# Before the expert rounds, GpSimd takes the last 512 of 2048 columns of the low-part subtraction that VectorE did alone

## What is computed

```python
def swiglu(h, w_gate, w_up, w_down):
    return (jax.nn.silu(h @ w_gate) * (h @ w_up)) @ w_down
```

## Time and profile before

| | |
|---|---|
| median of 3 runs | 2388.21 us (2387.69 to 2388.84) |
| span of the profiled execution | 2388.6 us |
| PE, DVE, ACT, POOL busy | 86%, 70%, 51%, 3% of the span |
| TensorE clock granted, mean | 0.915 of full speed |
| expert rounds begin | at about 1340 us |

### The profile page before, as it was taken

One profiled execution on the slowest core, in us unless ns is written; L12 is line 12 of the kernel. 1 busy time (PEld: TensorE's weight loads), 2 busy tenths in 40 slices (PEclk: granted clock), 3 DMA queues, 4 the chain that ended last, 5 costly groups with the idle time before them and its releaser, 6 DMA issues.

```text
span 2388.6 us, 26417 instructions
## 1 busy us (share of the span) xinstructions
PE 2044.1 (86%) x9364; PEld 1689.2 (71%) x9364; DVE 1672.2 (70%) x2143; ACT 1229.4 (51%) x1401; POOL 75.3 (3%) x112
## 2 busy tenths in 40 slices
PE   4876964868887878999875799999999999999998
PEld 3665853656665757888674687878878787878787
DVE  4764596565855574444464688878888888878787
ACT  3442112553443343344361476767677676767675
POOL 0200000120200100000000000000000000000000
PEclk8888986869987869999897799999999999999999
DMA  5430340412341423555441498989999898989795
GB/s 205 157 124 18 124 137 19 149 53 71 124 140 35 142 71 118 182 193 192 126 141 36 165 377 294 378 303 368 330 344 372 298 376 297 373 297 377 288 374 206
DMA packets 235620, 499.97 MB, mean 209 GB/s; under 512 B 9308, under 2 KB 41182, under 8 KB 235414
## 3 DMA queue, kind: packets, MB, share of 16 engines
q1 hardware_dynamic: 235024, 497.09, 58.9%
q10 hardware_dynamic: 518, 1.87, 0.2%
HBM read 497.88 MB, written 1.05 MB: 209 GB/s over the span
## 4 chain that ended last, share of the span: by engine, by line
PE 73%; DVE 18%; ACT 4%; issue 2%; POOL 1%; DMA 1%; SPq 0%; ACTq 0%; DVEq 0%; POOLq 0%
PE psum L732 22%; PE psum L734 22%; PE psum L733 22%; DVE arena L1493 4%; DVE low L717 3%; PE psum L2265 1%; ACT high L714 1%; PE psum L2349 1%; POOL small L909 1%; PE psum L2315 1%; DVE small L1147 1%; PE psum L1408 1%; DVE hT_low L894 1%; PE psum L2240 1%; ACT h L1095 1%
## 5 line engine op out<-in xcount | busy, mean ns | idle before, releaser
L717 DVE TENSOR_TENSOR low<-raw,high 128x2048 fp32r<-128x2048 f32 (+2 forms) x461 | 1049.0, 2281 | 435.1 <-ACT high L714 433.6
L714 ACT ACTIVATE high<-raw 128x2048 fp32r<-128x2048 f32 (+2 forms) x461 | 877.9, 1910 | 571.6 <-PE psum L734 511.1
L732 PE MATMUL psum<-high,yT_high 128*128 128x512 f32 x1672 | 676.3, 405 | 103.2 <-DVE yT_low L1527 46.4
L734 PE MATMUL psum<-high,yT_low 128*128 128x512 f32 x1672 | 665.6, 398 | 0.0
L733 PE MATMUL psum<-low,yT_high 128*128 128x512 f32 x1672 | 665.4, 398 | 0.0
L732 PEld LDWEIGHTS psum<-high,yT_high 128*128 128x128 f32 x1672 | 323.9, 194 | 181.7 <-issue 50.6
L734 PEld LDWEIGHTS psum<-high,yT_low 128*128 128x128 f32 x1672 | 323.5, 193 | 69.4
L733 PEld LDWEIGHTS psum<-low,yT_high 128*128 128x128 f32 x1672 | 324.5, 194 | 63.6
L732 PE MATMUL psum<-high,hT_high 128*128 128x512 f32 (+2 forms) x560 | 223.4, 399 | 43.1 <-DVE h L1355 19.7
L733 PE MATMUL psum<-low,hT_high 128*128 128x512 f32 (+2 forms) x560 | 220.4, 393 | 0.0
L734 PE MATMUL psum<-high,hT_low 128*128 128x512 f32 (+2 forms) x560 | 220.2, 393 | 0.0
(11 more groups left out here) (273 smaller groups left out, 1740.1 us busy)
## 6 DMA issues: line engine op xcount, KB each, us to landing
raw<-in_moe_w_gate SPq DMA_DIRECT2D x112, 1024.0 KB, 5.2
raw<-in_moe_w_up SPq DMA_DIRECT2D x112, 1024.0 KB, 5.4
raw<-in_moe_w_down SPq DMA_DIRECT2D x112, 1024.0 KB, 5.0
raw<-in_a_w_in SPq DMA_DIRECT2D x32, 1024.0 KB, 5.4
raw<-in_ffn_w_gate SPq DMA_DIRECT2D x14, 1024.0 KB, 5.1
raw<-in_ffn_w_up SPq DMA_DIRECT2D x14, 1024.0 KB, 5.1
raw<-in_ffn_w_down SPq DMA_DIRECT2D x14, 1024.0 KB, 4.9
raw<-in_b_w_in SPq DMA_DIRECT2D x12, 1024.0 KB, 5.0
```

Of the source, the lines that this page charges most:

```text
L714: eng.activation(high, raw, ACT.Copy).then_inc(k.high_ready, 1)
L717: eng.tensor_tensor(low, raw, high.bitcast(F32), ALU.subtract).then_inc(k.low_ready, 1)
L732: pe.matmul(out, lhs.high, rhs.high, start=start, stop=False)
L734: return pe.matmul(out, lhs.low, rhs.high, start=False, stop=stop)
```

## The change

`POOL_COLUMNS = 512`. Ahead of the rounds DVE subtracts the columns 0 to n - 512 of a granule of n columns and signals `low_ready`; POOL subtracts the last 512 and signals the new `low_end_ready`. Both wait for ACT's `high_ready`. PE waits for both signals ahead of a granule, and SyncE for both ahead of a load into the same raw buffer. POOL's programme gets calls of `ahead` at the same steps as ACT's and DVE's, in every layer but moe. In the rounds `split` keeps `end=0`, all columns on DVE.

```diff
 def ahead(k, eng, name):
-    engine = "act" if eng is k.nc.scalar else "dve"
+    engine = "act" if eng is k.nc.scalar else "pool" if eng is k.nc.gpsimd else "dve"
...
-            split(k, eng, n % SPLIT, g % RAW, granule.shape[0] * granule.shape[1], granule.number)
+            split(k, eng, n % SPLIT, g % RAW, granule.shape[0] * granule.shape[1], granule.number, POOL_COLUMNS)

-def split(k, eng, slot, raw_slot, n, number):
+def split(k, eng, slot, raw_slot, n, number, end=0):
     high, low, raw = k.high[:, slot, 0:n], k.low[:, slot, 0:n], k.raw[:, raw_slot, 0:n]
     if eng is k.nc.scalar:
         eng.activation(high, raw, ACT.Copy).then_inc(k.high_ready, 1)
+    elif eng is k.nc.gpsimd:
+        eng.wait_ge(k.high_ready, number + 1)
+        eng.tensor_tensor(low[:, n - end:], raw[:, n - end:], high[:, n - end:].bitcast(F32), ALU.subtract).then_inc(k.low_end_ready, 1)
     else:
         eng.wait_ge(k.high_ready, number + 1)
-        eng.tensor_tensor(low, raw, high.bitcast(F32), ALU.subtract).then_inc(k.low_ready, 1)
+        eng.tensor_tensor(low[:, 0:n - end], raw[:, 0:n - end], high[:, 0:n - end].bitcast(F32), ALU.subtract).then_inc(k.low_ready, 1)

 def wait_split(k, pe, g):
     pe.wait_ge(k.low_ready, k.granules[g].number + 1)
+    pe.wait_ge(k.low_end_ready, k.granules[g].number + 1)

@@ sync_weights
                 sp.wait_ge(k.low_ready, before.number + 1)
+                sp.wait_ge(k.low_end_ready, before.number + 1)

@@ load_round
         sp.wait_ge(k.low_ready, round_number(k, i - RAW, t) + 1)
+        if i < RAW:
+            sp.wait_ge(k.low_end_ready, round_number(k, i - RAW, 0) + 1)

 def norm_pool(k, pool, n):
     pool.wait_ge(k.ms_ready, 2 * n + 2)
     inverse_root(k, pool, k.ms, k.rstd, k.rstd_ready)
+    ahead(k, pool, ("norm", n, 3))

 def a_pool(k, pool, j):
     for i in range(8):
...
+        ahead(k, pool, (layer, "product", i))
         pool.wait_ge(k.group_ms_ready, n + 1)
...
+    for i in range(8, 16):
+        ahead(k, pool, (layer, "product", i))
+    ahead(k, pool, (layer, "scores", 0))

+def out_pool(k, pool, layer):
+    for name in out_names(layer):
+        ahead(k, pool, name)
```

More of the change, by code:

```diff
@@ L71 @@
 GROUP = 4
+POOL_COLUMNS = 512
 VECTOR_ROWS = {}
@@ L445, in __init__ @@
         self.engine_steps = {}
-        self.split_so_far = {"act": 0, "dve": 0}
+        self.split_so_far = {"act": 0, "dve": 0, "pool": 0}
         def sb(name, shape, dtype=F32):
@@ L522, in __init__ @@
         self.low_ready = sem("low_ready")
+        self.low_end_ready = sem("low_end_ready")
         self.half_done = sem("half_done")
@@ L1224, in attention_pool @@
             inverse_root(k, pool, k.out_ms[:, 0:GROUP], k.out_rstd[:, 0:GROUP], k.out_rstd_ready)
+    out_pool(k, pool, layer)
 def a_buffers(k, j):
@@ L1366, in a_pool @@
 def a_pool(k, pool, j):
+    layer = f"a{j}"
     for i in range(8):
-        n = GROUP_MS[f"a{j}"] + i
+        n = GROUP_MS[layer] + i
+        ahead(k, pool, (layer, "product", i))
         pool.wait_ge(k.group_ms_ready, n + 1)
         inverse_root(k, pool, k.group_ms[:, 8 * (i % 4):8 * (i % 4 + 1)], k.group_rstd[:, 8 * (i % 4):8 * (i % 4 + 1)], k.group_rstd_ready)
-    attention_pool(k, pool, f"a{j}")
+    for i in range(8, 16):
+        ahead(k, pool, (layer, "product", i))
+    ahead(k, pool, (layer, "scores", 0))
+    attention_pool(k, pool, layer)
 def b_buffers(k):
@@ L1739, in c_pool @@
     for kind, i in c_order():
+        ahead(k, pool, ("c", kind, i))
         if kind in ("low", "q", "kv"):
@@ L1745, in c_pool @@
             n += 1
+    ahead(k, pool, ("c", "scores", 0))
+    out_pool(k, pool, "c")
 def h_buffers(k):
@@ L1889, in h_pool, with b_pool, ffn_pool, r_pool @@
 def h_pool(k, pool):
[L1890 to L1893, removed]
+    n = 0
+    for kind, i in h_order():
+        ahead(k, pool, ("h", kind, i))
+        if kind in ("q", "kv"):
+            groups = H_HEADS if n < 2 else H_KV_HEADS
+            pool.wait_ge(k.group_ms_ready, GROUP_MS["h"] + n + 1)
+            inverse_root(k, pool, k.group_ms[:, 8 * n:8 * n + groups], k.group_rstd[:, 8 * n:8 * n + groups], k.group_rstd_ready)
+            n += 1
+    ahead(k, pool, ("h", "scores", 0))
+    out_pool(k, pool, "h")
+def b_pool(k, pool):
+    for i, kind, pair in b_products():
+        ahead(k, pool, ("b", "product", i))
+    ahead(k, pool, ("b", "squares"))
+    out_pool(k, pool, "b")
+def ffn_pool(k, pool):
+    for kind, j, t in ffn_order():
+        if kind != "down":
+            ahead(k, pool, ("ffn", kind, j, t))
+    out_pool(k, pool, "ffn")
+def r_pool(k, pool):
+    for kind, i in r_order():
+        ahead(k, pool, ("r", kind, i))
+    out_pool(k, pool, "r")
 def ffn_buffers(k):
@@ L2552, in _ @@
                     a_pool(k, pool, int(layer[1]))
-                elif layer in ("c", "h"):
-                    {"c": c_pool, "h": h_pool}[layer](k, pool)
+                elif layer != "moe":
+                    {"b": b_pool, "c": c_pool, "h": h_pool, "ffn": ffn_pool, "r": r_pool}[layer](k, pool)
 def store(k, sp, layers):
```

## The result

The changed kernel took 2401.16 us (median of 4 runs, 2400.56 to 2401.64) against 2388.24 us: 1.0053 times the kernel before, with a 95% interval of 1.0038 to 1.0067. Five later runs of the same kernel gave 1.0039 times (1.0026 to 1.0053). So it is slower by 0.4 to 0.5%, about 11 us. The forecast of 2395 had the sign and missed the median by 6 us, nearly as much as the loss that it forecast; the range of 2379 to 2408 held it.

What follows compares the result with a forecast made beforehand. The prediction saw TensorE busy for 86% of the span with 73% of the last chain, and 22 affected subtractions on the chain. Its place terms summed to +7 us on the 2388.21 median: 2395 us, range 2379 to 2408.

Steps and rivals of the forecast that it cites:

- free: Rival: DVE and POOL share nothing at this width, all 22 subtractions on the chain gain 0.53 us: -11, 2377 us; chance 0.10.
- (a): Attention layers a0 and a1, single subtraction, then reduction, then root, three on the chain in each: +0.1 us each, +0.6.
- (b): Pair of subtractions in a0 and its twin in a1: POOL subtracts while DVE still rotates, +1.4 us each, +2.8.
- (c): The subtraction ahead of each attention, where what follows reads PSUM: -0.5 us each, -1.0.
- (d): The subtraction ahead of a1's rope tables, which have two inputs: -0.53 + 1.25 = +0.7 us.
- (h): Two subtractions at the end of the feed-forward layer, each shorter by 0.53 us: -1.1.
- (e): Three subtractions of the convolution layer, inside an unbroken run of two-input taps: +3.7 - 1.6 = +2.1 us.
- (f): Latent attention: two stalled roots behind POOL's own subtraction, +0.7 us each, and -0.5 for a single one: +0.9.
- (g): Hybrid layer, its three subtractions: 0, +0.7 and about +0.2 us, +0.9 in the sum.
- (i): Recurrent layer: a conversion ends within the scan and product sequence leading to the output products: +1.2 us.
- One-sided: Rival: POOL waits for DVE, never DVE for POOL: about -6, 2382 us; chance 0.19.
- slow POOL: Rival: POOL takes 2.3 us an operation, some 19 places pay 1.05 us more each: +20 more, 2415 us; chance 0.12.

Runs made afterwards that it cites:

- pool_memset: The changed kernel, but POOL sets its 512 columns to zero without reading, waits kept, those low parts left out: 2377.52 us, 0.9946 times the kernel before.
- no_a: The changed kernel with the subtractions of the attention layers a0 and a1 given back whole to DVE: 2391.78 us, 1.0002 times the kernel before.
- only_b: The kernel before, with only the three subtractions inside the convolution layer's taps divided between DVE and POOL: 2390.96 us, 1.0008 times the kernel before.
- pool_extra: The changed kernel, but DVE subtracts all 2048 columns and POOL also the last 512, into its own buffer: 2411.29 us, 1.0089 times the kernel before.
- changed_again: The changed kernel word for word, run for a second profiled execution: 2400.9 us, 1.0039 times the kernel before.
- w1024: The changed kernel with 1024 columns on POOL, or half of a narrower granule, in place of 512: 2419.18 us, 1.0122 times the kernel before.

## Why the prediction was right in sign and 6 us off

**Part 1, DVE's gain.** The size is right, 0.53 us an operation, and the free case was put at -11: pool_memset, which is that case with all waits kept, is at -12.9. But the count of 22 places came near the total by luck. In c, with one place counted (0.5 us), the layer is 4.7 us shorter in pool_memset, with TensorE granted 0.85 of full speed there against 0.81 before; b, with three places (1.6), is 1.8 longer.

**Part 2, POOL's own time.** 1.25 us taken, 1.27 to 1.30 measured where POOL is first. The upper end of 2.3 is out. The estimate of 1.1 us from the Trainium skill, "GPSIMD Engine Reference", section "Performance versus the Vector engine", is lower than these rows, and equals what POOL needs behind DVE (2.87 less 1.76).

**Part 3, both ways.** The row that spoke against (a power passed by DVE's product) was rightly overruled. POOL first stops DVE for nearly its whole length: 2.88 us for 1.76. The order was right in most places, DVE first by 0.04 us; but in four (56.89, 449.92, 606.97 and 808.06) POOL was first by 0.02 to 0.03 with both idle, which I had excluded. Each costs DVE 1.1 us there.

**(a) and (b), the step that failed.** I put "Single subtraction, then reduction, then root (three on the chain in each of the layers a0 and a1)" at +0.1 each and let POOL be first only at "the pair at 66.64 and its twin in a1". The timeline shows POOL first, inside a rotation, at 614.61 (two), 628.03, 643.07 and 657.78 in a1, and at 64.50 (two), 77.90, 93.23 and 107.95 in a0: an item of these layers has two subtractions, and the conversion of the first is long done when POOL leaves its roots. The chain of before had shown only DVE's unbroken work there, so I had counted the second of each item and not the first. Each of the six single ones stops an addition for 0.96 us. The 0.53 us that DVE's subtraction behind the rotation saves isn't won: the item's second subtraction waits for ACT's conversion, for 0.5 us before (at 641.94 and 655.68) and for 1.0 in the changed kernel (at 650.76 and 665.49). The last of these, in the timeline of before and of the changed kernel:

```profile
655.68 2.29 DVE L717 TENSOR_TENSOR low<-raw,high 128x2048 fp32r<-128x2048 f32 x1 [0.52 <-ACT high L714]
...
665.49 1.76 DVE L724 TENSOR_TENSOR low<-raw,high 128x1536 fp32r<-128x1536 f32 x1 [1.04 <-ACT high L718]
```

So this second subtraction begins 1.0 us later by the one at 643.07 and another 1.0 by the one at 657.78, both counted from the same subtraction of the item in front; in a0 the ones at 93.23 and 107.95 do the same, and behind 77.90 and 628.03 nothing was lost in the first execution. The pair at 614.61 stopped the rotation for 1.35 us and not for the 2.5 that I had put, but the subtraction ahead of it (606.97) was one of those in which POOL is first and took 2.88 us where 2.29 were taken before. The working forecast +3.1 for both layers with (c) and (d); the profiles give +6.9 to +7.5, and no_a puts them at 9.1 of the total. This is the miss. The 2 us between the two are not placed; b's clock behind a0 may have a part in them.

**(c) and (h), the gain ahead of attention and at the end of the feed-forward layer.** (c) doesn't show by itself. (h), -1.1, was wrong: the layer is 252.9 us even in pool_memset, which has DVE's gain and no lock.

**(e), layer b.** +2.1 forecast, +0.17 measured in only_b. I had let all three POOL subtractions stop a tap for 1.25 us; two did, for 0.9 and 1.0.

**(f), (g), (i).** c +0.9 forecast, -1.2 and +0.1 in the two executions; h +0.9 forecast, +1.5 and +0.5; r +1.2 forecast, +0.3 and +1.6. No one of them is settled at this size. The mechanism of (f), a root behind POOL's own subtraction, is in the rows (451.34), and there DVE's stopped subtraction held the root up once more (1.58 us for 0.23).

**What was costed at nothing.** Right as far as it goes. PE waited for POOL's low part once, 5.8 us in all; the 40 subtractions inside the feed-forward layer cost nothing in one execution and at most 1.4 us in the other, though each of POOL's parts ended 1.1 us behind DVE's. TensorE's granted clock had no term in the sum at all.

**The rivals.** One-sided (2382) fell by the 2.88 us and by pool_extra; free (-11) is near what pool_memset measured once POOL no longer reads, and falls for the change itself; slow POOL (2415) had the wrong reason and the wrong size; hardly any effect (POOL at 0.7 us) fell by the 1.27 us and the loss of 9 to 13. That the total came within 6 us is in part luck: a0 and a1 lost 4 to 6 us more than forecast and the gain of 1.1 in ffn did not come, while b's own subtractions and c lost 1 to 2 us less each.

**The noise of a layer.** The prediction gave single layers to 0.1 us; two executions of one kernel differ by up to 4.6 us in a layer. What remains open is why the granted clock falls in one execution and not in the next.

## What to carry to other kernels

Here POOL was no second engine for work with two SBUF inputs beside DVE's own two-input work: the two took turns, and whoever started first delayed the other by nearly its whole remaining length. At 1.27 us for what DVE does in 0.53, the division loses where either engine is on the path. Before such a division, list for each operation when its input is ready and what DVE does from then on, not what stands beside it in the chain. And compare layers of two executions of the same kernel before a difference in one layer is explained.

## What the runs showed of the hardware

- The lock is mutual and nearly full: 2.87 us on POOL behind DVE's 1.76, 2.88 on DVE behind POOL's 1.27. DVE's reduction (one input) kept its 0.68 us beside POOL's subtraction, and POOL's memory set of 0.53 us ran inside DVE's subtraction.
- A run of DVE taps, each begun before the one ahead of it ended, kept a POOL operation of 1.27 us waiting for 17 us; at the first gap, of 0.04 us, it got in. The same gap let it in in the changed kernel (17.8 us), in changed_again (18.0) and in w1024 (19.2).
- POOL's time for a two-input subtraction where it is first and DVE idle: 0.73 us at 256 columns, 1.27 at 512, 2.35 to 2.40 at 1024. Begun inside a rotation of DVE's it is longer (0.92, 1.47 and 2.57 us).
- TensorE's granted clock gave layers of one kernel lengths that differ by 4.6 us in b (193.44 and 188.84), with spans 0.6 us apart.
